# Two transformer blocks on one core: the first expert unit is routed early, the opening is reordered, and VectorE sums three of the last rows

## The reference

```
shift1, scale1, gate1, shift2, scale2, gate2 = split(silu(c) @ w_ada[l] + b_ada[l])
h = rms_norm(x, norm1_g[l]) * (1 + scale1) + shift1
q, k, v, conv_x, conv_b, conv_c, pool_x = split(h @ w_in[l])          # 1024 x 1792
mix = concat(windowed attention(q, k, v), short conv, multiscale pool) @ w_out[l]
x = x + gate1 * mix
h2 = rms_norm(x, norm2_g[l]) * (1 + scale2) + shift2
q = h2 @ w_q                        # 8 heads of 256
s1, s2 = q_left @ keys[0].T, q_right @ keys[1].T      # 128 scores each
top 16 of each, top 16 of the 256 sums -> 16 experts per token and head, gate = softmax
y = sum over 128 experts of gate * gelu(h2 . expert_u[e]) * expert_v[e]
x = x + gate2 * y
```

## Time and profile before

| | |
|---|---|
| median of three runs | 2969.69 us (2968.46 to 2970.7) |
| profiled execution | 2969.69 us |
| its span in the profile | 2967.9 us |
| TensorE busy | 2428.5 us, 82% |
| VectorE busy | 1961.0 us, 66% |
| ScalarE busy | 770.4 us, 26% |
| GpSimd busy | 1054.7 us, 36% |
| DMA | 813 MB, mean 274 GB/s |
| first and last gather of layer 0 | 227.8 and 909.1 us |
| first and last gather of layer 1 | 1103.8 and 1785.0 us |

### The profile page before, as it was taken

One profiled execution on the slowest core, in us unless ns is written; L12 is line 12 of the kernel. 1 busy time (PEld: TensorE's weight loads), 2 busy tenths in 40 slices (PEclk: granted clock), 3 DMA queues, 4 the chain that ended last, 5 costly groups with the idle time before them and its releaser, 6 DMA issues. The chain is left out here.

```text
span 2967.9 us, 34182 instructions
## 1 busy us (share of the span) xinstructions
PE 2428.5 (82%) x11296; PEld 1721.5 (58%) x11296; DVE 1961.0 (66%) x3801; ACT 770.4 (26%) x1072; POOL 1054.7 (36%) x1122
## 2 busy tenths in 40 slices
PE   3788877777678788777677878998889989988898
PEld 3756333333235755333233336997779889987798
DVE  6774788887885844887888885556655534555554
ACT  2412000000011411000000003436543433444433
POOL 2304777777772305777777770002000000000000
PEclk7989888898889899898888989999999989999999
DMA  7676999999998647999999996663456544651564
GB/s 257 246 262 252 397 410 409 409 409 403 410 389 303 227 153 288 398 408 405 406 399 410 410 409 199 181 182 112 120 165 190 178 149 135 183 167 58 152 190 128
DMA packets 428303, 813.24 MB, mean 274 GB/s; under 512 B 28088, under 2 KB 266242, under 8 KB 428206
## 3 DMA queue, kind: packets, MB, share of 16 engines
q0 software_dynamic: 147968, 537.84, 45.8%
q1 hardware_dynamic: 280238, 274.15, 29.1%
HBM read 810.85 MB, written 1.05 MB: 274 GB/s over the span
## 5 line engine op out<-in xcount | busy, mean ns | idle before, releaser
L1478 PE MATMUL ps<-weight_ring,arena 128*128 128x512 f32 x2048 | 970.6, 635 | 320.2 <-DVE arena L2097 289.4
L1478 PEld LDWEIGHTS ps<-weight_ring,arena 128*128 128x128 f32 x2048 | 412.9, 205 | 877.5 <-issue 877.5
L2076 DVE CUSTOM_DVE_ANT_0 arena<-arena,ps 128x1024 f32<-128x1024 f32 x512 | 600.5, 1217 | 170.9 <-DMA arena<-in_peer_u,expert 170.2
L700 POOL DMA_INDIRECT arena<-in_peer_u,expert x512 | 483.8, 945 | 410.4 <-POOLq L699 205.5
L706 POOL DMA_INDIRECT weight_ring<-in_peer_v,expert x512 | 482.9, 943 | 161.5 <-issue 107.7
L1252 PE MATMUL ps<-hT_hi,ring_lo 128*128 128x256 f32 (+1 forms) x1856 | 531.0, 286 | 0.0
L1748 DVE TENSOR_TENSOR ring_lo<-weight_ring,w_hi 128x3072 fp32r<-128x3072 f32 (+1 forms) x104 | 332.1, 3194 | 256.3 <-DVEq L1747 256.2
L1250 PE MATMUL ps<-hT_hi,w_hi 128*128 128x256 f32 x1536 | 439.7, 286 | 15.7 <-PEq L1495 13.7
L1251 PE MATMUL ps<-hT_lo,w_hi 128*128 128x256 f32 x1536 | 439.0, 286 | 0.0
L1252 PEld LDWEIGHTS ps<-hT_hi,ring_lo 128*128 128x128 f32 (+1 forms) x1856 | 359.5, 194 | 0.0
L1250 PEld LDWEIGHTS ps<-hT_hi,w_hi 128*128 128x128 f32 x1536 | 299.3, 195 | 20.8 <-issue 17.5
(11 more groups left out here) (318 smaller groups left out, 3007.6 us busy)
## 6 DMA issues: line engine op xcount, KB each, us to landing
weight_ring<-in_w_ada SPq DMA_DIRECT2D x48, 1024.0 KB, 7.2
weight_ring<-in_ffn_w_gate SPq DMA_DIRECT2D x88, 512.0 KB, 4.0
weight_ring<-in_ffn_w_up SPq DMA_DIRECT2D x88, 512.0 KB, 5.3
weight_ring<-in_ffn_w_down SPq DMA_DIRECT2D x88, 512.0 KB, 5.8
weight_ring<-in_peer_wq SPq DMA_DIRECT2D x16, 1024.0 KB, 6.9
weight_ring<-in_w_in SPq DMA_DIRECT2D x12, 1024.0 KB, 11.2
weight_ring<-in_rg_w_in SPq DMA_DIRECT2D x12, 896.0 KB, 5.1
weight_ring<-in_w_out SPq DMA_DIRECT2D x8, 1024.0 KB, 10.3
```

The costliest lines, as they stand in the source:

```text
L700: g.indirect_dma_start(u_ring[:, k % U_SLOTS, :], None, A["peer_u"], bass.IndirectOffsetOnAxis(expert[:, p, k:k + 1], 0)).then_inc(u_in[k ...
L1478: ins = mm(ps[:, 2 * t + c, :], diag[:, k, :], v_place(l, k)[:, c * N:(c + 1) * N], start=False, stop=False, skip_group_check=True)
L2076: ins = v.tensor_tensor_reduce(out=u_ring[:, j, :], in0=u_ring[:, j, :], in1=h_rows(t), scale=1.0, scalar=0.0, op0=ALU.mult, op1=ALU.add, ...
```

## The change

- **Opening.** VectorE starts on SCALE1 at once; the rope angles and their two sines come later, beside the first blocks of `w_in`, and `window_share` comes after the rope. Both biases are loaded at the start. TensorE takes the first of SHIFT1's four parts by four matmuls with `c_act` spread as the stationary matrix. The weights of block 0 are split before `h` is ready, and TensorE may start on tile 0 when tile 0 is split.
- **Blocks.** `w_in` goes in seven blocks of 256 columns. `low_in(5)` now stands behind the fourth part of GATE1.
- **First unit.** `first_head(0)` forms head 0's query and keys of tile 0 before tile 1 is transposed, `first_head(1)` those of tile 1. VectorE routes unit 0 as soon as tile 0's keys are there. In layer 0, two parts of the next layer's SHIFT1 are done between the tiles and two after the routing. ScalarE does `gate_exp(0)` and `gelu(0)` behind query 3 and `gate_exp(1)` and `gelu(1)` behind query 7.
- **Last unit.** TensorE adds 13 rows, and VectorE sums the last three, weighs them with GATE2 and adds them to `x`; only then come its wait for `diag_free` and the slots.
- **Turn from layer 0 to 1.** ScalarE and VectorE split blocks 0 and 1 of layer 1 before VectorE waits for `y_ready`.

```
+            bias_row(0, SHIFT1, first_pad)
...
-                for b in range(8):
+                for b in range(IN_BLOCKS):
...
-                gate_exp(0)
-                with act.Fori(0, UNITS // 2 - 1) as n2:
-                    for p in range(2):
...
+                    if head == 3:
+                        gate_exp(0)
+                        gelu(0)
+                    if head == 7:
+                        gate_exp(1)
+                        gelu(1)
...
+            for k in range(2):
+                for c in range(2):
+                    ins = mm(ps[:, 2 + c, :], c_act[:, k:k + 1].to_broadcast([P, P]), ada_piece(SLOTS)[:, k, c * N:(c + 1) * N],
+                             start=(k == 0), stop=False)
...
+                turn_h_tile(0, WORK)
+                w_first = weights_in(0)
+                first_head(0, w_first)
+                turn_h_tile(1, WORK)
+                first_head(1, w_first)
...
+                later_part(3, mod[:, GATE1, :])
                 low_in(5)
-                later_part(3, mod[:, GATE1, :])
...
+                    if more and t == 0:
+                        for q in range(2):
+                            later_part(q, gain_post[:])
...
-                unit(1, UNITS - 1, 1, False)
+                unit(1, UNITS - 1, 1, False, LATE_ROWS)
+
+                beside = h[:, 1, :]
+                v.tensor_tensor(dots[:, 0, :], gate[:, GRP:TOPK], acts[:, 1, :], ALU.mult).then_inc(dve_steps, 1)
+                dve.wait_ge(dve_steps, steps.next())
+                for k in range(TOPK - LATE_ROWS, TOPK):
+                    dve.wait_ge(v_in[k], (l + 1) * UNITS * 16)
+                    if k == TOPK - LATE_ROWS:
+                        ins = v.tensor_scalar(beside, v_place(l, k), dots[:, 0, k - GRP:k - GRP + 1], None, ALU.mult)
+                    else:
+                        ins = v.scalar_tensor_tensor(beside, v_place(l, k), dots[:, 0, k - GRP:k - GRP + 1], beside, ALU.mult, ALU.add)
+                    ins.then_inc(dve_steps, 1)
+                    dve.wait_ge(dve_steps, steps.next())
+                    dve.sem_inc(v_free, 1)
+                v.tensor_tensor(beside, beside, mod[:, GATE2, :], ALU.mult).then_inc(dve_steps, 1)
+                dve.wait_ge(dve_steps, steps.next())
+                v.tensor_tensor(x[:, 1, :], x[:, 1, :], beside, ALU.add).then_inc(dve_steps, 1)
+                dve.wait_ge(dve_steps, steps.next())
                 dve.wait_ge(diag_free, 1)
                 for one in slot_free if more else slot_free[:SLOTS // 2]:
                     dve.sem_inc(one, 1)
+                if more:
+                    for u in range(2):
+                        low(u, in_hi, KC * BLK)
                 dve.wait_ge(y_ready, 1)
```

More of the change, by code:

```diff
@@ L470, in of, with load_in @@
                     return A[name][l]
+                w_in = of("w_in").rearrange("(k p) n -> p k n", p=P)
+                def load_in(u):
+                    load(u, [(0, P, KC, BLK, w_in[:, :, u * BLK:(u + 1) * BLK])])
+                for u in range(SLOTS):
+                    load_in(u)
                 sp.wait_ge(params_free, 1)
@@ L527, in _ @@
                         later_piece(l + 1, SHIFT1, q)
-                for head in range(SLOTS, EXPERT_HEADS):
+                for head in range(EXPERT_HEADS):
                     load_head(head)
@@ L1008, in gelu @@
                     a.activation(acts[:, half, :], dots[:, half, :], ACT.Gelu).then_inc(acts_ready, 1)
[L1010 to L1012 removed]
+                a.activation(h_rows(0), h[:, 0, :], ACT.Copy).then_inc(h_beside, 1)
+                query(1)
+                for head in range(2, EXPERT_HEADS):
+                    query(head)
+                    key_products(head - 1)
+                    if l + 1 < DEPTH and head == 3:
+                        spread(gain_post[:], 6)
+                    if head == 3:
[4 more added lines that the diff above has]
+                        gelu(1)
+                key_products(EXPERT_HEADS - 1)
+                act.sem_inc(key_s_ready, 1)
+                a.activation(h_rows(1), h[:, 1, :], ACT.Copy).then_inc(h_beside, 1)
+                with act.Fori(0, UNITS // 2 - 2) as n2:
+                    for p in (1, 0):
                         gelu(0)
@@ L1463, in _ @@
                     key_products(head - 1)
+                    if l + 1 < DEPTH and head == 3:
+                        pe.wait_ge(spread_taken, 1)
+                        pe.sem_inc(spread_taken, -1)
+                        spread(gain_post, 6, spread_for_act)
                 key_products(EXPERT_HEADS - 1)
@@ L2068, in _, with unit @@
                 best_pairs(0)
+                if more:
+                    dve.wait_ge(pre_in, 16)
+                    dve.sem_inc(pre_in, -16)
+                    scaled_gain(gain_pre[:], 6, gain_pre[:])
+                    dve.sem_inc(spread_taken, 1)
+                    for q in range(2, ADA_PAIRS):
+                        later_part(q, gain_post[:])
                 dve.sem_inc(dve_steps, -steps.reset())
-                def unit(t, n, p, follow):
+                def unit(t, n, p, follow, late=0):
                     for g in range(2):
@@ L2094, in unit @@
                         dve.sem_inc(diag_free, -1)
-                        for j in range(GRP):
+                        for j in range(GRP - (late if g == 1 else 0)):
                             k = g * GRP + j
```

330 lines of the change are left out of this document (186 added, 144 removed).

## The result

The changed kernel takes 2942.55 us (median of 6 runs, 2938.49 to 2947.29), the kernel before beside it 2970.74: a ratio of 0.9906, 95% interval 0.9893 to 0.9918. It is faster by 28 us where 40 were forecast, and lies within the range given. The profiled execution took 2940.9, its span is 2939.1: 28.8 less than before.

A forecast was written before the change was run, and what follows sets the result against it. Bounds: TensorE in the queries, gathers in the units, and a 21 us stretch waiting on ScalarE's late gelu and unit 1's routing. Terms -9.3 - 13.1 + 2.6 - 17.4 - 3.2 = -40.4 from 2969.69 gave 2929.3, range 2912 to 2948.

The forecast's parts named there:

- Opening and in-projection, -9.3: Layer 0's start: TensorE begins 10.3 us earlier, waits for blocks 4 and 5, and ends the in-projection 9.3 earlier.
- rival 1: In-projection: small loads don't hold block 4; layer 0's ends 6.5 us earlier, layer 1's 4: 2919; chance 0.16 with rival 3.
- Queries and first unit of layer 0, -13.1: Layer 0 from queries through the first unit: 11.3 us gained at unit 1's first v row, 1.8 in its loop.
- the v row, -11.3: Unit 1's first v row, waiting for v_free and TensorE's zeros, goes at 279 where it went at 290.3.
- rival 2: Early route only moves the idle: 5 of 13 us left in each layer, 2945; chance 0.20 with smaller such losses.
- the first unit's loop, -1.8: Layer 0's first unit: its loop of 42.8 us becomes 41.0.
- Turn, +2.6: Layer 0 to 1: slots behind the late rows issue w_in later; the in-projection loses 2.6 us (-5 to +5).
- rival 3: Turn to layer 1: w_in lands while VectorE still sums, 8 us better, 2921; chance 0.16 with rival 1.
- Layer 1, -17.4: Layer 1's queries and first unit: query 1 starts 4.7 us earlier, then -11.3 and -1.8 (-12 to -20).
- End, -3.2: End of layer 1: TensorE's rows save 5.2 us, feed-forward weights come later; first matmul 3.2 earlier (-5 to 0).
- Rival 4: Queries: TensorE runs at its lower level, 1.2 GHz, losing 50 us in each layer: 3029; chance 0.02.
- rival 5: Units: no change, if VectorE's loop rather than its start set the units' ends; chance 0.02.

The follow-up runs named there:

- gains_once: Changed kernel with q_norm_g and k_norm_g loaded once per partition, not once per head, and broadcast by VectorE: 2931.12 us, ratio 0.9862 to the kernel before.
- parts_mid: Changed kernel with layer 0's two SHIFT1 parts moved from between the tiles to behind tile 1's norm, ahead of unit 0's routing: 2935.17 us, ratio 0.9868.
- kp7_first: Changed kernel with ScalarE evacuating the last key scores ahead of gate_exp(1) and gelu(1), not behind them: 2932.60 us, ratio 0.9868.
- the control: The changed kernel unchanged, run again for comparison with the later follow-ups: 2946.07 us, ratio 0.9919 to the kernel before.
- slots_early_2: Changed kernel with slots given ahead of VectorE's three late rows: 2932.34 us, ratio 0.9867; as slots_early, on a chip with slower gathers, 3154.42 us, 0.9809.
- parts_after: Changed kernel with layer 0's two SHIFT1 parts moved from between the tiles to behind unit 0's routing: 2946.91 us, ratio 0.9909.
- gains_early: Changed kernel with loads of q_norm_g, k_norm_g and the sink moved ahead of GATE1's pieces, on a chip with slower gathers: 3157.89 us, ratio 0.9813.

## Why the prediction was right in kind and 12 us too high

**Opening and in-projection, -9.3: measured -8.1.** The order of the steps held. The first matmul came at 48.7 and not 47.0, since SHIFT1's first piece for VectorE landed at 24.9 and not 23.5; block 4's matmuls began at 77.4 and not 76.7. Block 5 waited for `low_in(5)`, but for 2.65 us and not 5.3: behind 4.42 us of idle block 4 took some 8.4 us, at a granted clock of 0.75, where 5.8 had been counted. That two errors nearly cancel here is luck. That the small loads hold block 4 was argued; gains_once shows it (5.7 us for 10.9), and rival 1 falls.

**Queries and first unit of layer 0, -13.1: measured -8.9.** This is the step that failed most, in three terms. First, "query 1 starts where it did": counted from the in-projection's end it started 2.1 late. Counted from the attention's end it is 3.7, for `w_out`'s last group began 9.7 us earlier (182.45, 172.77); those 1.6 us no term had, and in parts_mid they are not there. The parts held tile 1 longer than said: it was added 4.0 us earlier (189.73, 185.74), so 4.1 late by the in-projection and 5.7 by `w_out`, where 3.5 were forecast. And I had not gone on to what TensorE does in that time: it waits 4.40 us for ScalarE, which takes head 0's query only behind tile 1's norm, then 1.67 more, and does tile 1's half in 6.35 us, mostly at the lower level of 1.2 GHz, where I took 4.4. In parts_mid, with the parts elsewhere, both waits are below 1 us and the half takes 3.81. Second, the v row, -11.3: measured -10.4. It does hang on `v_free` and the zeros, as the forecast and rival 2 say, and kp7_first shows it: with one evacuation moved the idle falls from 9.45 us in the control to 4.61. Third, the first unit's loop, -1.8: measured -0.6. The 42.8 us had been counted from a u row and the gain from a v row; from v row to next unit it was 41.5 before.

**Units.** The period was 41.3 us from unit 2 to unit 14 (41.2 before), with a DMA share of 1.02 from 450 to 900 us, as before. From unit 2 to unit 15 the gain shrinks by 1.2 us in layer 0 and 1.3 in layer 1; nothing in the forecast had that, and no experiment was made for it.

**Turn, +2.6: measured +3.4** from unit 15's start to the end of layer 1's in-projection. The mechanism was right (slots_early_2: 7.1 us). Missed was that the last v rows take 8.8 us to land, so that the late rows begin at 899.7. Of rival 3 the runs say that it needs another order of the slots.

**Layer 1, -17.4: measured -16.6** at unit 2: -6.4 in the tiles and queries for -4.7, -9.3 for the v row, -0.9 for the loop. The three terms of the forecast, 4.7, 11.3 and 1.8, add up to 17.8; the sum was 0.4 off in itself.

**End, -3.2: measured -2.5**, and behind it 1.4 us are lost again in the unchanged part.

The misses add up: 1.2 + 4.2 + 1.2 + 0.8 + 0.8 + 1.3 + 0.7 + 1.4 = 11.6 = 40.4 - 28.8. Rival 4 got no support: the queries ran at 1.00. Nor did rival 5: the gain at unit 2 is kept to unit 15 but for 1.2 and 1.3 us. How the parts of the opening share its gain (the angles moved, the first part of SHIFT1 on TensorE, the splits ahead of `h`) was read from the timeline; no experiment takes them apart.

One thing that the sum did not need: the first late row took 0.75 us. The Trainium skill ("VectorE: DVE Perf Modes", "The perf-mode tier table") has a float32 `tensor_scalar` in SBUF at twice the rate of a two-tensor operation; against the 1.22 of those the trace agrees in the main, with 1.6 times.

The prediction held the rule on small pieces against the 16.7 us of `q_norm_g` and said that the trace disagrees. That was a misreading. The Trainium skill ("DMA: Bandwidth & Descriptors", "Why small descriptors are slow") gives 27% as the overhead within one piece of 256 bytes. From 54 to 62 us the 606 pieces took 7.1% of the time of sixteen engines, which is 15 ns for each; at the rate of 46 to 50 us (411 GB/s with a share of 1.03) 256 bytes would take about 10, by my estimate. So about a third of a piece's time is overhead, and the trace agrees with the rule roughly. What made the loads slow is that hardly more than one piece was moved at a time: 320 KB hold the queue for some 13 us.

## What to carry to other kernels

When a stall is filled with other work, follow what that work frees or holds: here two parts of a sum delayed tile 1, and at the same time emptied the slots that the next weights needed, so that the better place was neither where they stood nor behind all else. Before a late step is put ahead of giving a buffer back, see which part of the buffer it still reads. And an idle of 4 us before a short piece of TensorE's work cost 1.7 to 2.5 us more in the piece itself. Last, read what an edit is worth where the part that it touches ends: the unchanged rest of this kernel took from 1151 to 1162 us, more of a spread than some of the edits were worth.

## What the runs showed of the hardware

- Small broadcast loads left nearly all of the DMA engines idle: 320 KB in pieces of 256 bytes kept the DMA share at 0.07 for 8 us and longer, about what one engine of sixteen would give, and delayed a 1 MB load behind them by 5.2 us (10.9 for 5.7). A fifth of the pieces removed the delay, moving them did not.
- While gathers run, 1 MB of plain weights lands every 12.3 us (heads 4 to 7 in parts_after), where it takes 5.4 ahead of them (head 4 in parts_mid).
- TensorE's zeros: 3.70 us for eight instructions after 0.78 us idle (granted clock 1.00), 5.36 after 3.94 us idle (0.66). Half a head: 3.81 us at 1.00, and 6.35 at 0.57 behind idles of 4.40, 1.67 and 1.02.
- Chips differ: on one, gathers moved 348 and not 405 GB/s. There slots_early took only 3.5 us less than its neighbour gains_early, where elsewhere it took 13.7 less than the control, and leaving out the three late rows went with 11 to 15 us more (overlapping intervals), where elsewhere it made no difference.
